# A gated-linear-attention chunk loop: where ScalarE takes its second exponential and key copy, and where VectorE puts the second group's masked copy

## The reference

```python
o_inter = (q * exp(b)) @ S
att[t, s] = sum_d q[t, d] * k[s, d] * exp(b[t, d] - b[s, d])      # s <= t
o = o_inter + att @ v
S = exp(b_last) * S + (k * exp(b_last - b)).T @ v
...
out = (rms_norm(o) * silu(r)) @ w_out
```

## Time and profile before

| | us |
|---|---|
| median of 3 runs | 2412.05 |
| lowest and highest | 2410.3, 2419.3 |
| profiled execution, its own time | 2416.19 |
| its span | 2414.5 |
| mean granted clock of TensorE | 0.966 |

### The profile page before, as it was taken

One profiled execution on the slowest core, in us unless ns is written; L12 is line 12 of the kernel. 1 busy time (PEld: TensorE's weight loads), 2 busy tenths in 40 slices (PEclk: granted clock), 3 DMA queues, 4 the chain that ended last, 5 costly groups with the idle time before them and its releaser, 6 DMA issues.

```text
span 2414.5 us, 29324 instructions
## 1 busy us (share of the span) xinstructions
PE 2278.6 (94%) x12340; PEld 1959.7 (81%) x12340; DVE 1077.5 (45%) x1309; ACT 667.7 (28%) x1035; POOL 867.6 (36%) x501
## 2 busy tenths in 40 slices
PE   7999989899999999989999979899999999999898
PEld 7999967899998888868887658777877777777676
DVE  2899988500067766630026555222122222222643
ACT  3454351112245642210136634100000000000243
POOL 2789731332245535023275440333223223222100
PEclk9999989999978889999999989999999999999899
DMA  3111114211100023211220022121111111111211
GB/s 126 53 36 53 54 52 131 74 53 32 39 1 1 1 70 131 88 53 35 106 75 2 1 88 96 44 70 53 35 52 51 35 52 43 44 52 61 105 64 50
DMA packets 89610, 136.61 MB, mean 57 GB/s; under 512 B 6464, under 2 KB 71616, under 8 KB 89374
## 3 DMA queue, kind: packets, MB, share of 16 engines
q1 hardware_dynamic: 89502, 135.08, 16.6%
HBM read 118.26 MB, written 16.81 MB: 56 GB/s over the span
## 4 chain that ended last, share of the span: by engine, by line
PE 76%; POOL 8%; DVE 7%; ACT 4%; issue 4%; DMA 2%; SPq 0%; DVEq 0%; POOLq 0%; ACTq 0%
PE PS L359 61%; PE PS L2004 3%; PE PS L1047 2%; PE PS L1081 2%; PE PS L399 2%; POOL side_sum L539 2%; PE PS L2313 1%; PE PS L388 1%; PE PS L1675 1%; POOL pool_tmp L1899 1%; PE PS L1662 1%; PE PS L1688 1%; POOL arg_b L1270 1%; POOL arg_b L1269 1%; POOL mo_raw L1924 1%
## 5 line engine op out<-in xcount | busy, mean ns | idle before, releaser
L359 PE MATMUL PS<-xh,wh 128*128 128x512 f32 (+2 forms) x1664 | 523.3, 364 | 11.1 <-DVE xl L454 4.0
L359 PE MATMUL PS<-xl,wh 128*128 128x512 f32 (+2 forms) x1664 | 519.0, 362 | 0.0
L359 PE MATMUL PS<-xh,wl 128*128 128x512 f32 (+2 forms) x1664 | 517.0, 361 | 0.0
L342 POOL CAST wh<-raw 128x2048 fp32r<-128x2048 f32 x46 | 87.3, 1897 | 821.7 <-PE PS L359 737.5
L359 PEld LDWEIGHTS PS<-xh,wh 128*128 128x128 f32 x1664 | 312.0, 189 | 50.5 <-issue 5.8
L359 PEld LDWEIGHTS PS<-xl,wh 128*128 128x128 f32 x1664 | 311.8, 189 | 40.9
L359 PEld LDWEIGHTS PS<-xh,wl 128*128 128x128 f32 x1664 | 311.2, 189 | 39.7
L337 POOL TENSOR_TENSOR wl<-raw,wh 128x2048 fp32r<-128x2048 f32 x62 | 287.5, 4637 | 53.1 <-ACT wh L333 49.4
L359 PE MATMUL PS<-wh,xh 128*128 128x256 f32 (+1 forms) x784 | 229.5, 317 | 2.7 <-DVE wl L350 0.9
L359 PE MATMUL PS<-wl,xh 128*128 128x256 f32 (+1 forms) x784 | 228.4, 316 | 0.0
L359 PE MATMUL PS<-wh,xl 128*128 128x256 f32 (+1 forms) x784 | 227.9, 316 | 0.0
(11 more groups left out here) (331 smaller groups left out, 3460.6 us busy)
## 6 DMA issues: line engine op xcount, KB each, us to landing
h_rows<-rows SPq DMA_DIRECT2D x24, 512.0 KB, 2.6
rows<-h_rows SPq DMA_DIRECT2D x24, 512.0 KB, 3.3
raw<-in_w_ffn_down_dram SPq DMA_DIRECT2D x11, 1024.0 KB, 4.8
raw<-in_gla_w_in_dram SPq DMA_DIRECT2D x10, 1024.0 KB, 5.1
raw<-in_w_ffn_gate_dram SPq DMA_DIRECT2D x10, 1024.0 KB, 5.0
raw<-in_w_ffn_up_dram SPq DMA_DIRECT2D x10, 1024.0 KB, 5.0
raw<-in_conv_w_in_dram SPq DMA_DIRECT2D x16, 512.0 KB, 4.7
raw<-in_w_in_dram SPq DMA_DIRECT2D x8, 1024.0 KB, 5.5
```

Of the source, the lines that this page charges most:

```text
L342: nc.gpsimd.tensor_copy(wh[slot][:], buf[:]).then_inc(unit_hi, 1)
L359: last = nc.tensor.matmul(out_of(c, cn), s, x[:, c0:c0 + cn], start=n == 0 and m == 0, stop=n == len(terms) - 1 and m == 2)
```

## The change

On ScalarE, `factors` of the second group moves from behind the exponential for the decayed queries to behind the two silus, one chunk iteration earlier (it is called for chunk c+1 at the end of iteration c). The key copy moves from behind the output copy to ahead of the four output squares, also written one iteration earlier. On VectorE, `weights` of the second group no longer stands behind all four levels of the next chunk's first exponents but between levels 0 and 1 and levels 2 and 3. No instruction is added or dropped.

```diff
 for c, (c0, n) in enumerate(TILES):                 # gla_scalar
-    if 0 < c < NX:
-        copy_keys(act, c)
     if c > 0:
         nc.scalar.activation(q_decayed[:], decay[:], ACT.Exp, scale=1 / TAU).then_inc(qdec_exp, 1)
-        factors(act, c, 1)
...
             nc.scalar.activation(r_silu[h][:], r_out(c, h), ACT.Silu).then_inc(r_left, 1)
+    if c < NX:
+        factors(act, c + 1, 1)
+    if 0 < c + 1 < NX:
+        copy_keys(act, c + 1)
     if c > 0:
         act.wait_ge(o_done, c)
...
-def exponents(c, g):
+def exponents(c, g, levels):
...
-    for g in range(2):                              # gla_vector
-        if c > 0:
-            weights(c, g)
...
-        if c < NX:
-            exponents(c + 1, g)
+    if c > 0:
+        weights(c, 0)
+    if c < NX:
+        exponents(c + 1, 0, GROUPS[0][:2])
+    if c > 0:
+        weights(c, 1)
+    if c < NX:
+        exponents(c + 1, 0, GROUPS[0][2:])
...
+    if c < NX:
+        exponents(c + 1, 1, GROUPS[1])
```

More of the change, by code:

```diff
@@ L1194, in exponents @@
                 after(dve, pair_done, 2 * (c - 2) + g + 1)
-                for l in GROUPS[g]:
+                for l in levels:
                     x, e = halves(decay[:], l), halves(level_arg(l), l)
@@ L1200, in exponents @@
                     last = nc.vector.tensor_tensor(e[:, :, 1, :], x[:, :, 1, :], ref, ALU.subtract)
-                last.then_inc(arg_ready, 1)
+                if levels[-1] == GROUPS[g][-1]:
+                    last.then_inc(arg_ready, 1)
             def weights(c, g):
@@ L1228, in gla_vector @@
                     sums(c + 1)
-                for g in range(2):
-                    if c > 0:
-                        weights(c, g)
[L1232 to L1235, removed]
-                    if c < NX:
-                        exponents(c + 1, g)
+                if c > 0:
[6 more added lines that the diff above has]
+                    exponents(c + 1, 0, GROUPS[0][2:])
+                if c == 0:
+                    dve.wait_ge(unit_ready, U_GR + 1)
+                    dve.wait_ge(gv_tile, GH * NV_TILES)
+                    split_unit_fast(dve, U_GR + 1, 1)
+                if c < NX:
+                    exponents(c + 1, 1, GROUPS[1])
                 if c < NX:
```

## The result

| | before | changed |
|---|---|---|
| median of 11 runs each, us | 2411.57 | 2423.01 |
| lowest and highest, us | 2409.46, 2419.30 | 2414.37, 2431.64 |
| profiled execution, its own time, us | 2416.19 | 2424.31 |
| its span, us | 2414.5 | 2422.6 |
| mean granted clock | 0.966 | 0.961 |

The ratio of the changed kernel to the one before is 1.0037, 95% interval 1.0022 to 1.0052: slower by 5 to 13 us, or 0.37%. In the profiled executions the difference is 8.1 us of span. The loop holds 3.5 of them. Another 3.2 lie ahead of it: the first state products start at 675.69 us instead of 672.50, in code that the change doesn't touch. The last 1.4 lie behind the loop.

What follows compares the result with a forecast made beforehand. Bound: the chain ScalarE, GpSimd, TensorE, with half clock behind TensorE's idling. Terms -1 + 1.7 + 3.5 = +4 on the profiled 2416.2 gave 2420, stated as 2419.5, 7 above the median; range 2403 to 2431.

Steps and rivals of the forecast that it cites:

- Second exponential: Step 1, ScalarE: moved behind the silus, it ends TensorE's 2.26 us wait for `arg_b`; `o_kept` is late next.
- Key copy: Step 2, ScalarE: ahead of the squares, it puts the output copy's end at +5.8 us earliest; TensorE waits at least 1.1.
- Masked copy: Step 3, VectorE: between the halves, it releases the first exponential at about 803.8 instead of 801.88 us; ScalarE's later work follows.
- Short and long chunks: Six middle chunks: 21.3 and 30.3 us alternating, or all 27.3; 155 or 164 against 159.1, weighted gain 1.
- First chunk: Loop start: key copy behind the exponential makes the gate logits wait, +1.7 us.
- Last chunk: Loop's last chunk: later `o_kept` and half clock over seven levels, +3.5 us on average with the chance of a short one.
- The half clock in every chunk: Slower rival, loop: clock falls at each first group, no chunk short, six at 28 us; 2432 us, chance 0.22.
- The clock holds: Faster rival, loop: no alternation, idling costs only itself, chunks of 22.5 us; 2392 us, chance 0.10.
- Nothing moves: Rival, loop: clean alternation and a short last chunk, the fall gives the gain back; 2408 to 2412 us, chance 0.12.
- The rule: Skill's section ties the clock's fall to idle gaps longer than any in middle chunks; by it every changed chunk is short.

Runs made afterwards that it cites:

- e3_exp_keys: Kernel before with both ScalarE moves (second exponential, key copy), VectorE's order the old one: 2411.27 us, ratio 0.9994 to the kernel before.
- e1_dve_only: Kernel before with only VectorE's masked copy moved between the halves of the first exponents: 2414.57 us, ratio 1.0006 to the kernel before.
- e8_first_keys: Changed kernel, but chunk 1's key copy stands ahead of its second exponential as before: 2416.46 us, ratio 1.0015 to the kernel before.
- e10_best_no_fill: Kernel before with both ScalarE moves, chunk 1's keys as before, old VectorE order, no `r` products moved ahead: 2407.95 us, ratio 0.9967.
- e2_exp_only: Kernel before with only the second exponential moved behind the silus: 2410.18 us, ratio 0.9981 to the kernel before.
- e9_exp_dve: Kernel before with second exponential and masked copy moved, key copy left behind the output copy: 2430.98 us, ratio 1.0059 to the kernel before.
- e7_best: Kernel before with both ScalarE moves, old VectorE order, chunk 1's keys as before, 12 `r` products ahead of the first group: 2399.15 us, ratio 0.9933.
- e5_after_spare: Changed kernel with 18 useless matmuls per chunk added before the first group: 2402.48 us, ratio 0.9948 to the kernel before.
- e6_before_spare: Kernel before with 20 useless matmuls added before the second group, where TensorE waited for `arg_b`: 2410.16 us, ratio 0.9983.

## Why the prediction was right, and where it was off

The direction, the mechanism and, within a few us, the time came as forecast. The forecast was the likeliest case, 2419.5 us, +7 on the median; measured are 2423.0, +11.4, or +9 by the ratio. Step by step:

1. *Second exponential.* Right. No wait for GpSimd at `arg_b` is left. What was late next was the line to `o_kept`, as said.
2. *Key copy.* Right. The waits before the first group are 0.92 to 0.93 us behind a long chunk (forecast: at least 1.1) and 2.88 in all behind a short one (forecast: some 3).
3. *Masked copy.* Right in mechanism, but only behind a short chunk: there the squares start 5.1 to 5.2 us after the last output product, against 3.2 in e3_exp_keys, which lacks the masked copy's move (forecast: first exponential some 2 us later). Behind the other chunks up to the sixth they start after 3.06 in both kernels. That it was harmless without the other two, e1_dve_only, the prediction didn't say, since it took the edits together.
4. *Short and long chunks.* Measured 21.2 and 20.7 for the short (forecast 21.3), 27.1 for the long (27 to 28), 30.6 and 30.8 for a long one behind a short (30.3). Two short ones came where strict alternation of the six would give three; three chunks stayed at 27.1. The six took 153.7 us against 159.1: -5.3, where the sum has -1. It was mis-sized by the weighting of the two patterns, two to one, which no row supported; the pure alternation had been worked out as 155.
5. *First chunk.* Term +1.7, measured +3.0. The step took the key copy's later start as the end of its effect. The copy started where forecast, 1.39 us behind the exponential's start, but the logits wait for its end:

```profile
681.05 1.48 ACT L1133 ACTIVATE arg_b<-arg_b 128x1536 f32<-128x1536 f32 x1 [5.41 <-DVE arg_b L1201]
682.44 0.57 ACT L1106 COPY k_rows<-PS 128x512 f32<-128x512 f32 x1
...
683.05 2.08 PE L1019 MATMUL PS<-a,w_a 33*128 33x128 f32 x8 [3.18 <-ACT k_rows L1106]
```

   From the loop's first state product the logits start at +7.36 instead of +5.15, so 2.2 us of the 3.0. The other 0.8 fits the stretch of 0.50, which lies later (to +27.4 instead of +23.3) and so covers more of the `r` products; that part is argued, not measured apart. The term itself hangs on the execution: with the old order at the start the first chunk took 29.3, 24.9, 24.9 and 29.3 us (before, e1_dve_only, e8_first_keys, e10_best_no_fill), against 32.1 to 32.3 with the key copy behind the exponential: some 3 to 7 us.
6. *Last chunk.* Term +3.5, measured +6.0: 30.8 us, since a short chunk came ahead of it. The prediction's own figure for that case, 30.3, is right within half a microsecond; the term was an average over both cases. e2_exp_only and e3_exp_keys had a long one ahead and took 18.1.

The sum of the terms is -5.3 + 3.0 + 6.0 = +3.7, against +4. That the sum agrees so well is luck in part: the two terms that were too small and the gain that was too small offset each other. The loop itself, up to the next stage's first product, grew by 3.5, since 0.3 us less lie behind its last output product. These 3.5 us are also only part of the 8.1 between the two executions and of the 9 to 11 between the medians. The medians differ by more than the loops of the two profiled executions, and the latter vary: e2_exp_only's took 4.7 us less than its median, e10_best_no_fill's 7.3 more. The prediction put the whole effect into the loop and said nothing of what varies around it. That the time goes with the granted clock is on record (the 74 executions above), and two causes are likely: the clock falls at other places around the loop, and the first chunk is slow in every execution instead of in some. No run shows the pattern of an execution without a profile, and how the missing 5 to 8 us divide stays open.

**The rivals.** "The half clock in every chunk", 2432, has the time of e9_exp_dve (2430.98), but not its way there: in that kernel too two chunks (21.0 and 20.8) stayed at 1.00. Its pattern of one long chunk after the other stands in the profiled execution of e10_best_no_fill, five of 27.1. "The clock holds", 2392, is what e7_best and e5_after_spare come near to, once TensorE has work at that spot. "Nothing moves", 2408 to 2412 by clean alternation and a short last chunk, did not come for the changed kernel, whose loop grew by 3.5 us where this rival has it shrink by 5. It describes e2_exp_only, which alternated cleanly, had a last chunk of 18.1 and took 2410.18 (0.9981).

**The rule.** The clock fell behind idle stretches of 2.26 us before, and in the changed kernel behind 0.92, 0.93, and 1.10 + 1.78 us (the rows at 765.96, 793.02 and 737.35). By the section "HAM oscillation — how this bites in real kernels" of the Trainium skill's "TensorE: Matmul & The Clock Gate", which asks for longer idle gaps, it should have held in all these chunks. The trace disagrees, in both kernels, and the measurement decides. But the length of the idle stretch alone doesn't decide either: behind 2.76 us the clock held once in e6_before_spare, and behind 1.10 in e5_after_spare.

## What to carry to other kernels

Before an instruction is moved up on an engine, follow what it pushes back to the next buffer release (here the output copy), and price that release by what the waiting engine has to do behind it: a wait ahead of seven levels of pair products costs more than a longer one ahead of three or of none. Where a wait can't be avoided, put work that doesn't depend on it there; twelve to twenty `r` products moved ahead of the wait were worth 0.3 to 0.8%, while the three reorderings cost 0.37% together. Two moves that measure as nothing or as a small gain (1.0006, 0.9981) cost 0.59% together (1.0059), so the combination has to be run too. And before a loop's length is set against a median, see how much the code around the loop varies; here it was some 10 us.

## What the runs showed that was not expected

- 144 useless matmuls made a kernel 20 us faster (e5_after_spare).
- Five rows of 0.92 to 0.93 us of idling, alike in what stands around them, were followed by half clock in three chunks and not in two (793.02 fell, 847.16 held). In e6_before_spare the same holds for two waits of 2.76 us (804.54 fell, 831.52 held). And the kernel before fell to 0.50 at 675.3, at the loop's start, with no idle stretch over 0.53 us in the 25 us ahead. What decides is not in these rows and stays open.
- Once fallen at the first group, the clock stayed at 0.50 for 13.6 to 17 us while TensorE was busy all the time with the pair products (767.9 to 781.5, busy 13.60 of 13.60).
- The masked copy's move is worth nothing alone, costs 0.78% beside the second exponential, and again nothing once TensorE has its filling (0.9936 against 0.9933).
